# Row tiles scaled and transposed by products with diagonal matrices, and the first input weights split between the row tiles

## What is computed

```python
def rmsnorm(x, g):
    y = x * lax.rsqrt(jnp.mean(x * x, axis=-1, keepdims=True) + RMS_EPS)
    return y * g

h = rmsnorm(x, norm_mix_g)
proj = h @ w_in                                   # 1024 x 1536
u_rnn, g_rnn, u_pool, q_mem = split(proj)
y_mem = memory_cross_attention(q_mem, rmsnorm(mem, mem_norm_g), w_mem_kv)
```

## Time and profile before

| | us |
|---|---|
| median of 3 runs | 1797.6 (1797.19 to 1801.99) |
| the profiled execution, its time | 1800.14 |
| its span, first to last instruction | 1798.1 |
| TensorE busy in it | 1692.6 |
| VectorE, ScalarE, GpSimd busy | 1331.5, 1092.3, 537.8 |

### The profile page before, as it was taken

How to read it: one execution, slowest core, us unless ns; L and a number is a source line. 1 busy time by engine, 2 the same in 40 slices (tenths; PEclk the granted TensorE clock), 3 DMA queues, 4 the chain that set the end, 5 groups by cost and what they waited for, 6 DMA issues and landing times.

```text
span 1798.1 us, 29154 instructions
## 1 busy us (share of the span) xinstructions
PE 1692.6 (94%) x8545; PEld 1257.1 (70%) x8546; DVE 1331.5 (74%) x1137; ACT 1092.3 (61%) x1044; POOL 537.8 (30%) x379
## 2 busy tenths in 40 slices
PE   4998979958999999999999999999999999999897
PEld 4776758846578677888877887668667667665573
DVE  6487755557579696989978899669668668764685
ACT  5234265436478576868867687657556657663573
POOL 5233130232132261522323323125213126222244
PEclk9999989968999999999999999999999999999898
DMA  8310122248788889999989998889868788787675
GB/s 263 94 35 24 43 80 90 95 147 341 271 325 333 306 323 346 378 392 392 385 316 359 372 398 326 299 326 373 311 266 287 289 337 324 282 294 276 227 283 201
DMA packets 114072, 485.85 MB, mean 270 GB/s; under 512 B 16319, under 2 KB 28929, under 8 KB 81249
## 3 DMA queue, kind: packets, MB, share of 16 engines
q1 hardware_dynamic: 96016, 445.58, 64.0%
q0 software_dynamic: 18000, 39.49, 9.1%
HBM read 451.79 MB, written 33.23 MB: 270 GB/s over the span
## 4 chain that ended last, share of the span: by engine, by line
PE 70%; DVE 4%; issue 2%; DMA 1%; ACT 1%; POOLq 0%; DVEq 0%; ACTq 0%; POOL 0%; SPq 0%
PE ps L1674 19%; PE ps L1676 18%; PE ps L1675 18%; PE ps L1689 6%; PE ps L1727 3%; DVE w_lo L1520 2%; PE ps L1647 2%; PE ps L1697 1%; PE ps L1752 1%; DMA raw_weights<-in_w_down 1%; ACT w_hi L1376 1%; DVE raw_weights L1621 1%; DVE raw_weights L1636 0%; PE ps L1656 0%; DMA stand_in<-token_lists 0%
## 5 line engine op out<-in xcount | busy, mean ns | idle before, releaser
L1520 DVE TENSOR_TENSOR w_lo<-raw_weights,w_hi 128x2048 fp32r<-128x2048 f32 x256 | 577.0, 2284 | 140.2 <-ACT w_hi L1376 140.1
L1376 ACT ACTIVATE w_hi<-raw_weights 128x2048 fp32r<-128x2048 f32 x256 | 485.6, 1911 | 225.8 <-DMA raw_weights<-in_w_gu 115.1
L1674 PE MATMUL ps<-w_hi,xT 128*128 128x512 f32 x1024 | 416.7, 407 | 17.5 <-issue 10.6
L1675 PE MATMUL ps<-w_lo,xT 128*128 128x512 f32 x1024 | 404.3, 395 | 0.9 <-issue 0.9
L1676 PE MATMUL ps<-w_hi,xT 128*128 128x512 f32 x1024 | 403.6, 394 | 0.0
L1520 DVE TENSOR_TENSOR w_lo<-raw_more,w_hi 128x2048 fp32r<-128x2048 f32 x128 | 290.1, 2285 | 29.8 <-ACT w_hi L1376 29.8
L1674 PEld LDWEIGHTS ps<-w_hi,xT 128*128 128x128 f32 x1024 | 194.8, 190 | 98.2 <-issue 48.4
L1296 POOL DMA_INDIRECT x_rows<-h_rows,next_list x33 | 78.5, 2379 | 616.8 <-issue 616.8
L1376 ACT ACTIVATE w_hi<-raw_more 128x2048 fp32r<-128x2048 f32 x128 | 244.0, 1907 | 1.4 <-DMA raw_more<-in_w_down 1.4
L1676 PEld LDWEIGHTS ps<-w_hi,xT 128*128 128x128 f32 x1024 | 194.6, 190 | 42.9
L1675 PEld LDWEIGHTS ps<-w_lo,xT 128*128 128x128 f32 x1024 | 195.1, 190 | 38.7 <-issue 1.7
(11 more groups left out here) (296 smaller groups left out, 2262.6 us busy)
## 6 DMA issues: line engine op xcount, KB each, us to landing
raw_weights<-in_w_gu SPq DMA_DIRECT2D x192, 1024.0 KB, 9.1
raw_more<-in_w_gu SPq DMA_DIRECT2D x64, 1024.0 KB, 6.6
raw_weights<-in_w_down SPq DMA_DIRECT2D x64, 1024.0 KB, 9.3
raw_more<-in_w_down SPq DMA_DIRECT2D x64, 1024.0 KB, 12.0
rows<-in_x SPq DMA_DIRECT2D x12, 512.0 KB, 6.1
w_in_sb<-in_w_in SPq DMA_DIRECT2D x12, 512.0 KB, 4.1
raw_weights<-in_w_out SPq DMA_DIRECT2D x1, 4096.0 KB, 13.4
acc_rows<-region_c SPq DMA_DIRECT2D x8, 512.0 KB, 2.7
```

The lines of the kernel that those rows point to most:

```text
L1376: S.activation(w_hi[:, j % RING, :], raw(j % RING), ACT.Copy).then_inc(hi_done, 1)
L1520: V.tensor_tensor(w_lo[:, j % RING, :], raw(j % RING), w_hi[:, j % RING, :].bitcast(F32), ALU.subtract).then_inc(lo_done, 1)
L1674: T.matmul(out, hi, hi_w, start=first, stop=False)
L1675: T.matmul(out, hi, lo_w, start=False, stop=False)
```

## The change

Row tiles are no longer scaled on VectorE. ScalarE multiplies the identity by a tile's reciprocals (new `row_scale` on ScalarE, 128x128), which gives a diagonal matrix, one of two in turn, in the place of `b_gu_lo`. TensorE computes, for each of the eight blocks, the product of the block as it is (stationary) with this diagonal (moving), in plain fp32, in place of the transpose against the identity: it gives the transposed and scaled block. ScalarE makes the high part of the first bank only; VectorE makes that of the second itself, by a copy. Roots and reciprocals run one tile ahead. The table of the square root is loaded at the very start.

The first two blocks of w_in are scaled by GpSimd ahead of its fillings and clearing DMAs, as soon as the gain is there, and the gain comes one tile earlier (TensorE transposes it ahead of tile 2 and not of tile 3, VectorE copies it out in turn 3 and not 4). ScalarE makes their high parts in turns 5 and 7, VectorE the low parts in turns 6 and 8. The two halves of the first projection stand between the tiles: half 0 behind tile 7, half 1 behind tile 8. SyncE takes the three blocks of w_in and row tiles 7 to 9 by turns.

```diff
...
         b_gu_lo = sb("b_gu_lo", [P, 2, HALF], F32R)
+        scales = nc.alloc_sbuf_tensor_at("scales", [P, 2, P], F32, offset=start["b_gu_lo"])
...
             sem(n) for n in ("b_gu_in", "b_gu_hi_done", "b_gu_lo_done", "bias_set", "const_set", "pick_done"))
+        rs_done = sem("rs_done")
         dve_step, pool_step = sem("dve_step"), sem("pool_step")
...
                 load_w_in(n)
-            for item in range(len(row_slots), NORMED):
-                sp.wait_ge(xT_ready, item - len(row_slots) + 1)
-                load_rows(item)
+                sp.wait_ge(xT_ready, n + 1)
+                load_rows(len(row_slots) + n)
             sp.wait_ge(xT_ready, len(row_slots))
...
+            pool.wait_ge(vec_done, 1)
+            def scale(n):
+                pool.wait_ge(w_in_in[n % 3], ring_value(n, 3))
+                nc.gpsimd.tensor_tensor(w_in_sb[:, n % 3, :, :], w_in_sb[:, n % 3, :, :],
+                                        vec[:, V_GMIX:V_GMIX + KT].unsqueeze(2).broadcast_to([P, KT, P]), ALU.mult)\
+                    .then_inc(w_in_scaled, 1)
+
+            scale(0)
+            scale(1)
             pool.memset(r_pad, 0.0).then_inc(zero_set, 1)
...
-            pool.wait_ge(vec_done, 1)
-            def scale(n):
-                pool.wait_ge(w_in_in[n % 3], ring_value(n, 3))
-                nc.gpsimd.tensor_tensor(w_in_sb[:, n % 3, :, :], w_in_sb[:, n % 3, :, :],
-                                        vec[:, V_GMIX:V_GMIX + KT].unsqueeze(2).broadcast_to([P, KT, P]), ALU.mult)\
-                    .then_inc(w_in_scaled, 1)
-
             def w_in_lo(n):
...
-            for n in range(NPROJ):
+            for n in range(2, NPROJ):
                 scale(n)
...
                 act.wait_ge(xT_ready, s + 1)
-                for b in range(2):
-                    nc.scalar.activation(hi_part[:, 4 * b:4 * b + 4, s * P:(s + 1) * P],
-                                         bank(4 + 2 * (s % 2) + b)[:, 0, :].rearrange("p (k t) -> p k t", k=4),
-                                         ACT.Copy).then_inc(x_hi_done, 1)
+                nc.scalar.activation(hi_part[:, 0:4, s * P:(s + 1) * P],
+                                     bank(4 + 2 * (s % 2))[:, 0, :].rearrange("p (k t) -> p k t", k=4),
+                                     ACT.Copy).then_inc(x_hi_done, 1)
+
+            def row_scale(s):
+
+                if s >= 2:
+                    act.wait_ge(xT_ready, s - 1)
+                act.wait_ge(rs_done, s + 1)
+                nc.scalar.activation(scales[:, s % 2, :], ident[:, :], ACT.Copy, scale=rs[:, s:s + 1]).then_inc(xn_done, 1)
...
+            act.preload_act_table(ACT.Sqrt)
             square(0)
             square(1)
+            act.wait_ge(consts, 1)
+            root(0)
             for s in range(NORMED):
-                root(s)
+                if s + 2 < NORMED:
+                    square(s + 2)
+                if s + 1 < NORMED:
+                    root(s + 1)
+                row_scale(s)
                 if 1 <= s <= TT:
                     x_hi(s - 1)
-                if s + 2 < NORMED:
-                    square(s + 2)
-                if s == TT - 1:
-                    w_in_hi(0)
-            w_in_hi(1)
+                if s == 5 or s == 7:
+                    w_in_hi((s - 5) // 2)
             act.wait_ge(lam_abs, 1)
...
                 dve.wait_ge(sd_done, s + 1)
-                link(V.reciprocal(rs[:, s:s + 1], sd[:, s:s + 1]))
-                V.tensor_scalar(row_tile(s), row_tile(s), rs[:, s:s + 1], None, ALU.mult).then_inc(xn_done, 1)
+                V.reciprocal(rs[:, s:s + 1], sd[:, s:s + 1]).then_inc(rs_done, 1)
...
-                        dve.wait_ge(x_hi_done, 2 * s + b + 1)
                         at = (slice(None), slice(4 * b, 4 * b + 4), slice(s * P, (s + 1) * P))
+                        if b:
+                            link(V.tensor_copy(hi_part[at], src))
+                        else:
+                            dve.wait_ge(x_hi_done, s + 1)
                         V.tensor_tensor(lo_part[at], src, hi_part[at].bitcast(F32), ALU.subtract).then_inc(xT_done, 1)
...
             mean_square(0)
+            mean_square(1)
+            row_scale(0)
             for s in range(NORMED):
-                row_scale(s)
                 if s + 1 < NORMED:
-                    mean_square(s + 1)
+                    row_scale(s + 1)
+                if s + 2 < NORMED:
+                    mean_square(s + 2)
+                if s == 3:
+                    vector_columns()
+                    dve.wait_ge(vec_done, 1)
                 if s:
                     xT_evac(s - 1)
-                if s == 4:
-                    vector_columns()
-                    dve.wait_ge(vec_done, 1)
-                if s == TT:
-                    w_in_lo(0)
+                if s == 6 or s == 8:
+                    w_in_lo((s - 6) // 2)
             xT_evac(NORMED - 1)
-            w_in_lo(1)
...
             pe.wait_ge(consts, 1)
-            for s in range(NORMED):
-                if s == 3:
-                    pe.wait_ge(vrows_in, 16 * 8)
-                    T.transpose(bank(0)[:, 0, 0:V_N], vrows[0:V_N, :], ident[0:V_N, 0:V_N]).then_inc(vecT_ready, 1)
+
+            def transpose_rows(s):
+
                 pe.wait_ge(xn_done, s + 1)
...
                 for k in range(KT):
-                    last = T.transpose(bank(4 + 2 * (s % 2) + k // 4)[:, 0, (k % 4) * P:(k % 4 + 1) * P],
-                                       row_tile(s)[:, k * P:(k + 1) * P], ident[:, :])
+                    last = T.matmul(bank(4 + 2 * (s % 2) + k // 4)[:, 0, (k % 4) * P:(k % 4 + 1) * P],
+                                    row_tile(s)[:, k * P:(k + 1) * P], scales[:, s % 2, :], start=True, stop=True)
                 last.then_inc(xT_ready, 1)
-            def project(n):
+            def project_half(n, h):
...
                 w_hi, w_lo = (w_in_split[n % 2][:, i, :, :] for i in range(2))
+                if n == 0:
+                    pe.wait_ge(xT_done, 2 * 4 * (h + 1))
+                    pe.wait_ge(vec_done, 1)
+                if n == 2 or n == 3:
+                    pe.wait_ge(u_done if n == 2 else gelu_done, h + 1)
+                elif 4 <= n < 2 * RT + 2:
+                    c = (n - 2) // 2
+                    pe.wait_ge(u_done if n % 2 == 0 else gelu_done, 2 * c + h + 1)
+                elif n >= 2 * RT + 2:
+                    pe.wait_ge(pu_done, 2 * (n - 2 * RT - 2) + h + 1)
+                acc, cols = bank(2 * (n % 2) + h)[:, 0, :], slice(h * HALF, (h + 1) * HALF)
+                for k in range(KT):
+                    T.matmul(acc, w_hi[:, k, :], hi_part[:, k, cols], start=(k == 0), stop=False)
+                    T.matmul(acc, w_hi[:, k, :], lo_part[:, k, cols], start=False, stop=False)
+                    last = T.matmul(acc, w_lo[:, k, :], hi_part[:, k, cols], start=False, stop=(k == KT - 1))
+                last.then_inc(proj_ready, 1)
+
+            def project(n):
                 for h in range(2):
-                    if n == 0:
-                        pe.wait_ge(xT_done, 2 * 4 * (h + 1))
-                        pe.wait_ge(vec_done, 1)
-                    if n == 2 or n == 3:
-                        pe.wait_ge(u_done if n == 2 else gelu_done, h + 1)
-                    elif 4 <= n < 2 * RT + 2:
-                        c = (n - 2) // 2
-                        pe.wait_ge(u_done if n % 2 == 0 else gelu_done, 2 * c + h + 1)
-                    elif n >= 2 * RT + 2:
-                        pe.wait_ge(pu_done, 2 * (n - 2 * RT - 2) + h + 1)
-                    acc, cols = bank(2 * (n % 2) + h)[:, 0, :], slice(h * HALF, (h + 1) * HALF)
-                    for k in range(KT):
-                        T.matmul(acc, w_hi[:, k, :], hi_part[:, k, cols], start=(k == 0), stop=False)
-                        T.matmul(acc, w_hi[:, k, :], lo_part[:, k, cols], start=False, stop=False)
-                        last = T.matmul(acc, w_lo[:, k, :], hi_part[:, k, cols], start=False, stop=(k == KT - 1))
-                    last.then_inc(proj_ready, 1)
+                    project_half(n, h)
+
+            for s in range(NORMED):
+                if s == 2:
+                    pe.wait_ge(vrows_in, 16 * 8)
+                    T.transpose(bank(0)[:, 0, 0:V_N], vrows[0:V_N, :], ident[0:V_N, 0:V_N]).then_inc(vecT_ready, 1)
+                transpose_rows(s)
+                if s >= TT - 1 and s < NORMED - 1:
+                    project_half(0, s - TT + 1)
...
             for c in range(RT):
-                project(2 * c)
+                if c:
+                    project(2 * c)
                 project(2 * c + 1)
```

## The result

The changed kernel takes 1789.55 us (median of 18 runs, 1771.17 to 1793.87), the kernel before 1797.18 in the same sessions (18 runs, 1793.71 to 1801.99). The ratio is 0.9947, 95% interval [0.9934, 0.9961]: 9.5 us faster, 7.0 to 11.9; by the two medians it is 7.6. The forecast was 6.2 us. The direction was right and the size too small: even the lower end of the interval is above it.

The account below looks back on a forecast made before the run. TensorE, busy 94% of the span, was held up in front by the row tiles' chain across engines. Tiles to 33.2 us, then projection halves with tiles 8 and 9, gave 48.1 against 54.28: 6.2 us gained, 1791.4, range 1788.5 to 1793.

Parts of the forecast that it names:

- Where the gain lies: Time won before the second projection (54.28 us) moves the whole rest, as long as it stays under some 15 us.
- Start: Tile 0's products start at 10.0 us, 0.6 later than before; rows 2 arrive at 8.43, the table load brings nothing.
- TensorE per tile: Eight diagonal products, 16 records a tile, take 3.6 us at the low clock and 1.9 at the high one.
- rival C: Weight load and stream add up on TensorE, 6.8 and 3.5 us a tile; 8.7 us slower, 1806; chance 0.04.
- Which clock: TensorE runs tiles 0 and 1 at the low clock, 10.0 to 17.2 us, then high; one low tile only is 1.3 better.
- Rival B: TensorE's clock stays low through the tiles, 3.6 us each; 1.0 us slower, 1798.6; chance 0.17.
- The rule weighed there: Trainium skill: transposes in transpose mode do not count as busy for TensorE's clock, so products replacing them would raise it.
- VectorE per tile: A VectorE turn takes 2.4 us and sets the pace from tile 2 on; ScalarE needs 2.2 at most.
- GpSimd stall: VectorE's mean square waits some 1.8 us beside GpSimd's second w_in product, near 22.7 us; may be 0 or 3.8.
- SP: Row tiles 7 to 9, issued from 13.7 us by turns with w_in loads, arrive late; 1.6 us of loss at 11 to 12 latency.
- rival D: Gain real but only 2 to 5 us, from late rows, full GpSimd stall, longer VectorE turns or late gates inputs; 1794; chance 0.23.
- The sum: Front's terms add to a second projection at 48.1 us instead of 54.28, 6.2 us gained; median 1791.4.

Follow-up runs that it names:

- the last experiment: Changed kernel with the first diagonal ahead of square 2, plus both high parts of tiles 0, 2, 4 and 6 on ScalarE; ratio 0.9919.
- the probe: Changed kernel plus two small VectorE scalings with unused results, 128x2 in turn 4 and 128x4 in turn 8; 1791.8 us.
- the old order: Changed kernel with SyncE loading all three w_in blocks ahead of row tiles 7 to 9; 1789.98 us.
- the repeat of the old scaling: Second run of the changed kernel with VectorE's 1024-column scaling and transposes against the identity restored; ratio 0.9961.

## Why the prediction was right or wrong

*Where the gain lies: right.* It was placed in front of the second projection, and 8.43 of its 8.52 us arrive at the gates. No earlier input took the gates over.

*Start: right.* 10.09 for 10.0. The table load now runs from 0.95 and brought nothing here, since row tile 2 still arrived at 8.41. That it arrives then "whatever is changed" was luck: in one later trace it was there by 7.18, and tile 0 began at 8.86. That the order costs the start some 2.4 us was implicit in this step (the diagonal stands behind square 2), and the kernel with the first diagonal ahead shows it.

*TensorE per tile: right in kind and size.* The high-clock tile costs 1.70 to 1.78 us from start to start (36.82 to 38.52, 29.46 to 31.24), below the 1.9. Load and stream don't add up: rival C is out.

*Which clock: size off.* Two low tiles were taken, 17.2; the 32 records took 5.84 and ended at 15.9, so the clock rose inside tile 1, between the two bounds. 1.3 us better, of which 0.5 was lost again to the first hole, 0.62 before tile 2. Rival B is out. The rule weighed there is contradicted, though its consequence, that the clock would rise here, came true for the other reason.

*VectorE per tile: nearly right, for a partly wrong reason.* Tiles 2 to 7 start (29.46 - 16.75)/5 = 2.54 us apart instead of 2.4. VectorE alone does not set this pace, as the last experiment shows. I had said that the high parts of w_in fall in turns in which ScalarE is ahead; it wasn't, and tile 6 waited 1.00 us for its diagonal. Five turns cost 0.7 us more than forecast.

*GpSimd stall: wrong.* 1.8 us were charged, 0 came. That "VectorE's mean square has the same engine, operation and SBUF operands as the stalled scaling" was true and not enough: what separates them is the width, by the 0.13 and 2.56 us of the probe. The lower bound of that term was the case. In the sum the turns from tile 2 to tile 7 were 13.8 with the stall and took 12.71.

*SP: cost less than the 1.6 us held ready for rival D*; even the old order costs only what the 0.68 us wait does, and the second projection came 0.2 us later.

*The sum.* Tile 2 started 0.75 earlier than forecast (17.5), the turns from tile 2 to 7 saved 1.09, tile 7 0.12, the two halves with tiles 8 and 9 took 14.52 instead of 14.9: 0.75 + 1.09 + 0.12 + 0.38 = 2.34, which is 48.1 less 45.76. The failed terms are the GpSimd stall (1.8) and the second low tile (1.3), set off by 0.7 in the turns. 6.2 + 2.3 is the front's 8.5, inside the measured 7.0 to 11.9. The forecast had both bounds: its low end, 1788.5, is one low tile and no stall, and both came true. The front's 8.5 alone would give 1789.1; the last us to the ratio's 1788.1 no term of the sum holds.

*What the forecast did not separate* is which part wins. By the marks at the gates: the division and the earlier parts of w_in alone 5.8 us; adding roots ahead and the new loads 5.5, no more; the products make it 8.2 to 8.8, as they take the wide scaling off VectorE (of wide operations between SBUF tiles only the low parts of w_in stay there, and in the change they ran in 1.22 us), and the dense tiles bring half 0 the high clock (8.23 us for 24 matmuls in the repeat of the old scaling against 5.58 in the change). The shares don't add: beside the products the division is worth 1.3 to 1.6. GpSimd's order is worth 0.4 alone and, counted from tile 0's start, about 1 beside the products. Most of these are single traces.

*The total against the front.* 9.5 us by the ratio, 8.5 at the front. The difference is inside the interval, and the stages behind vary by more than that from run to run with identical code. The low tail, which the kernel before's 65 runs lack, leaves it open whether the last us is chance.

## What to carry to other kernels

Where VectorE and GpSimd share a stage, move wide operations between SBUF tiles off VectorE rather than reorder GpSimd: a reorder moved the stall to the next wide operation, while the products took ten of twelve such operations away, and the front came out alike in four traces. The two that are left can still be hit, as the probe showed. A chain of short turns ahead of a long matmul block is best ended by dividing the block, so that the last turns lie beside its halves; try that part alone first, since here it held two thirds of the gain. When the rest of a kernel varies by more than the change is worth, compare one mark behind the changed stage, in more than one trace.

## What the runs showed of the hardware

- A 128x1 fp32 scaling on VectorE ran in 0.13 us beside a GpSimd product that held a 128x2 one for 2.56 us, through the filling that followed.
- The hold can last through back-to-back GpSimd operations: 5.7 to 6.4 us for a scaling that takes 0.75 alone, in all four traces in which three products ran in a row beside it; a subtraction that takes 1.22 took 2.0 to 4.2. The Trainium skill (SBUF — State Buffer, SBUF: two separate sides) speaks of the pair being held for one instruction. Here three products in a row held it to their end, while beside two products a scaling came through after the first (2.30 us).
- Dense fp32 transposes reach the high clock (16 records in 1.97 us), single ones sometimes (8 in 1.10) and sometimes not (8 in 1.97).
- The granted clock is written as full until its first fall in a trace, a low start included: in the kernel before 1.00 from 40 to 45 us, where matmuls of 512 columns start 0.43 us apart. Behind a fall it agrees with the pitch: 0.50 from 31 to 37 us in the repeat of the old scaling. At the start of a trace the pitch is the better witness.
- The same expert code took 1369.5 to 1387.1 us from one execution to the next, 1381 or more in 13 of 16 traces.
